# RWKV recurrence on one Trainium2 core: order of the next slot's Gram product, and the engine that masks and copies t1

## The reference, cut to what matters

```python
def frame_step(state, inp):
    r_t, w_t, k_t, v_t, a_t, b_t = inp
    sa = jnp.einsum('bhvk,bhk->bhv', state, a_t)
    state = (state * w_t[:, :, None, :]
             + sa[..., None] * b_t[:, :, None, :]
             + v_t[..., None] * k_t[:, :, None, :])
    y_t = jnp.einsum('bhvk,bhk->bhv', state, r_t)
    return state, y_t
```

## Time and profile before

| | |
|---|---|
| median of 3 runs | 1352.33 us (1350.98 to 1352.74) |
| profiled execution, first to last instruction (the page gives no other time of it) | 1350.7 us |
| PE matmul, weight load | 97%, 84% of the span |
| VectorE, ScalarE, POOL | 70%, 52%, 9% |
| granted TensorE clock | 0.998 |

### The profile page before, as it was taken

How to read it: one execution, slowest core, us unless ns; L and a number is a source line. 1 busy time by engine, 2 the same in 40 slices (tenths; PEclk the granted TensorE clock), 3 DMA queues, 4 the chain that set the end, 5 groups by cost and what they waited for, 6 DMA issues and landing times. The chain is left out here.

```text
span 1350.7 us, 24951 instructions
## 1 busy us (share of the span) xinstructions
PE 1303.9 (97%) x10507; PEld 1130.7 (84%) x10507; DVE 948.4 (70%) x1433; ACT 701.1 (52%) x1211; POOL 128.3 (9%) x133
## 2 busy tenths in 40 slices
PE   4999999999999999999999999999999999999997
PEld 2998888997899887788888887888888998888886
DVE  1887788976768776685556888666657677756655
ACT  2534544434467455564444648654445566644443
POOL 0000000010200864100000142000000021000000
PEclk9999999999999999999999999999999999999999
DMA  9997899995341012356665532465565544565561
GB/s 363 373 366 236 302 350 381 356 344 161 110 156 64 4 35 97 98 178 196 188 192 177 176 121 74 150 203 192 187 196 160 170 143 126 172 188 192 183 197 51
DMA packets 177559, 256.90 MB, mean 190 GB/s; under 512 B 10472, under 2 KB 122536, under 8 KB 177448
## 3 DMA queue, kind: packets, MB, share of 16 engines
q1 hardware_dynamic: 177448, 255.31, 57.0%
HBM read 254.25 MB, written 1.05 MB: 189 GB/s over the span
## 5 line engine op out<-in xcount | busy, mean ns | idle before, releaser
L1507 DVE TENSOR_TENSOR w_lo<-stage,w_hi 128x1024 fp32r<-128x1024 f32 (+1 forms) x372 | 447.3, 1238 | 160.4 <-ACT w_hi L882 160.0
L882 ACT ACTIVATE w_hi<-stage 128x1024 fp32r<-128x1024 f32 (+1 forms) x378 | 379.9, 1049 | 211.7 <-PE acc L2311 191.9
L2309 PE MATMUL acc<-w_hi,z_hi 128*128 128x512 f32 x640 | 252.7, 395 | 1.6 <-DVE z_lo L1956 1.6
L2311 PE MATMUL acc<-w_hi,z_lo 128*128 128x512 f32 x640 | 249.4, 390 | 0.0
L2310 PE MATMUL acc<-w_lo,z_hi 128*128 128x512 f32 x640 | 249.2, 389 | 0.0
L2252 PE MATMUL un<-h_both,w_hi 128*128 128x256 f32 x736 | 214.9, 292 | 1.8 <-POOL w_lo L853 1.1
L2253 PE MATMUL un<-h_both,w_hi 128*128 128x256 f32 x736 | 208.8, 284 | 0.0
L2254 PE MATMUL un<-h_both,w_lo 128*128 128x256 f32 x736 | 208.8, 284 | 0.0
L2252 PEld LDWEIGHTS un<-h_both,w_hi 128*128 128x128 f32 x736 | 141.6, 192 | 9.5 <-issue 5.4
L2309 PEld LDWEIGHTS acc<-w_hi,z_hi 128*128 128x128 f32 x640 | 120.1, 188 | 27.8 <-issue 3.9
L2253 PEld LDWEIGHTS un<-h_both,w_hi 128*128 128x128 f32 x736 | 141.7, 193 | 1.2 <-issue 0.7
(11 more groups left out here) (393 smaller groups left out, 1885.1 us busy)
## 6 DMA issues: line engine op xcount, KB each, us to landing
stage<-in_mlp_w SPq DMA_DIRECT2D x64, 1024.0 KB
ada_buf<-in_ada_w SPq DMA_DIRECT2D x48, 1024.0 KB, 11.1
stage<-in_w_up SPq DMA_DIRECT2D x32, 1024.0 KB
stage<-in_w_down SPq DMA_DIRECT2D x32, 1024.0 KB
stage<-in_conv_w_in SPq DMA_DIRECT2D x12, 1024.0 KB
stage<-in_rw_w_rkv SPq DMA_DIRECT2D x12, 1024.0 KB
stage<-in_w_in_a SPq DMA_DIRECT2D x8, 1024.0 KB
stage<-in_w_kv_b SPq DMA_DIRECT2D x8, 1024.0 KB
```

Of the source, the lines that this page charges most:

```text
L882: A_(w_hi[u % 2][:, half, 0:n], stage[u % NSTAGE][:, half, 0:n], ACT.Copy).then_inc(hi_made, 1)
L1507: V.tensor_tensor(w_lo[u % 2][:, half, 0:n], stage[u % NSTAGE][:, half, 0:n], w_hi[u % 2][:, half, 0:n].bitcast(F32), ALU.subtract).then_i ...
L2309: MM(y, z_hi[:, kt, q], wh[:, i, :], start=(first and kt == 0), stop=False, skip_group_check=True)
L2311: ins = MM(y, z_lo[:, kt, q], wh[:, i, :], start=False, stop=(last and kt == KT - 1), skip_group_check=True)
```

## The change

1. gram is taken apart into gb, start, nb, vt, gk and nk. gb, start (VectorE: level 0 mask, unit added, two turns, for both q at once) and nb (both causal masks, both q at once, 1024 columns) of slot s+1 are steps of slot s: in slots 1 and 2, gb goes ahead of level 5 and start and nb between its t1 and its dx. In slot 0 they follow dx(5,1). gk writes the same two banks as gb, and its masks (nk) are one instruction too, put between dx(2,0) and dx(2,1).
2. The Gram block itself, nb_t, is now t1's left operand at every level, in acc[2], acc[3]. The level's mask is put on the product by VectorE when it copies t1. n_m, POOL's products and ScalarE's t1 copies are gone.
3. The order of the first two levels is mixed with vt, gk and tok; ScalarE's bk_tok copies move from level 1 to level 2; the chain's places are new.
4. keep_y moves from VectorE to ScalarE, behind the copy of u. Places of the beside and group steps are named by step instead of by number. POOL loses its n_m products, and its builds stand first in its list.
5. Elsewhere (near 806 us) a semaphore keys_chosen is replaced by VectorE's own link. The fourth slot's inverse gets a tile of its own.

```diff
-        wkv_prepare = [("gram", 0, 0), ("gram", 0, 1), ("tok", 0, 0), ("tok", 0, 1)]
-        for j in WKV_LEVELS:
+        wkv_prepare = [("vt", 0, 0), ("t1", 1, 0), ("t1", 1, 1), ("gk", 0, 0), ("dx", 1, 0), ("tok", 0, 0), ("dx", 1, 1),
+                       ("t1", 2, 0), ("tok", 0, 1), ("t1", 2, 1), ("dx", 2, 0), ("nk", 0, 0), ("dx", 2, 1)]
+        for j in (3, 4):
             wkv_prepare += [("t1", j, 0), ("t1", j, 1), ("dx", j, 0), ("dx", j, 1)]
-        WKV_CHAIN_AFTER = (0, 1, 1, 5, 6, 8, 11, 12, 14, 16, 18, 20)
+        LAST_LEVEL = [("t1", 5, 0), ("t1", 5, 1), ("dx", 5, 0), ("dx", 5, 1)]
+        NEXT_GRAM, NEXT_START, NEXT_NB = ("gb", 0, 0), ("start", 0, 0), ("nb", 0, 0)
+        LAST_STEPS = ([*LAST_LEVEL, NEXT_GRAM, NEXT_START, NEXT_NB],
+                      [NEXT_GRAM, *LAST_LEVEL[0:2], NEXT_START, NEXT_NB, *LAST_LEVEL[2:4]])
+        WKV_CHAIN_AFTER = (0, 2, 3, 6, 8, 10, 12, 14, 16, 18, 20, 23)
...
+        GROUP_PE = {**{s: {("t1", 3, 1): ("bonus", s - 2), ("dx", 3, 1): ("var", s - 2)} for s in (2, 3)},
+        GROUP_ACT = {**{s: {("t1", 2, 0): (("square", s - 2),), ("t1", 4, 0): (("shift", s - 2),),
+                            ("t1", 4, 1): (("ln", s - 2), ("exp", s - 2), ("square_root", s - 2))} for s in (2, 3)},
+        GROUP_DVE = {**{s: {("dx", 3, 1): (("bonus", s - 2),), ("dx", 4, 1): (("add_eps", s - 2),), ("start", 0, 0) if s == 2 else ("t1", 5, 1): (("root", s - 2),),
+                            ("dx", 5, 1): (("scale", s - 2),)} for s in (2, 3)},
+        CROSSED_AT = ((("dx", 3, 1), ("dx", 4, 1)), (("dx", 4, 0), ("t1", 5, 1)))
+        SPLIT_HIGH = {(0, ("t1", 4, 1)): 0, (0, ("t1", 5, 1)): 1, (1, ("rhs", 2, 0)): 0, (2, ("rhs", 2, 0)): 1}
+        SPLIT_LOW = {(0, ("dx", 4, 1)): 0, (0, ("dx", 5, 1)): 1, (1, ("u", 2, 0)): 0, (2, ("u", 2, 0)): 1}
...
 (POOL)
-                for j in WKV_LEVELS[1:]:
-                        G.tensor_tensor(n_m[(j - 1) % 2][:, q, :, :], nb_t[s % 2][:, q, :, 0:CHUNK],
-                                        level_t[:, j, :].unsqueeze(1).to_broadcast([P, CHUNKS, CHUNK]), ALU.mult).then_inc(nm_ready, 1)
...
 (ScalarE)
                     elif step == "t1":
-                        act.wait_ge(t1_done, 10 * s + 2 * (j - 1) + q + 1)
-                        A_(t1[:, q, :, :], half_bank(acc[q], 0), ACT.Copy).then_inc(t1_out, 1)
-                        if j == 1:
+                        if j == 2:
                             act.wait_ge(tok_done, s + 1)
                             A_(bk_tok[SLOT_SET[s]][:, q, :, :, :].rearrange("p b c s -> p (b c s)"), flat(un[q]), ACT.Copy).then_inc(tok_out, 1)
...
                         A_(wkv_u[:], two_pairs(stat_ps, P), ACT.Copy).then_inc(u_out, 1)
+                        if j:
+                            keep_y(s, j - 1)
+                    elif step == "sy" and j == CHUNKS - 1:
+                        keep_y(s, j)
...
 (VectorE)
+                    if step == "start":
                         dve.wait_ge(g_done, s + 1)
+                        link(V.tensor_tensor(inv_of[s][:], gram_first[:, :, :, 0:CHUNK], in_pairs(level_first), ALU.mult))
+                        link(V.tensor_tensor(inv_of[s][:], inv_of[s][:], in_pairs(eye), ALU.add))
+                        for m in range(2):
+                            if s:
+                                dve.wait_ge(t1_done, 10 * s - 2 + m + 1)
+                            V.transpose(in_line(inv_x[:, m, :, :]), in_line(inv_of[s][:, m, :, :])).then_inc(start_ready, 1)
+                    elif step == "nb":
+                        if s >= 2:
+                            dve.wait_ge(y_done, CHUNKS * (s - 1))
+                        V.tensor_tensor(nb_t[s % 2][:], gram_first, in_pairs(c_("masks")), ALU.mult).then_inc(masked, 1)
+                    elif step == "nk":
                         dve.wait_ge(gk_done, s + 1)
+                        V.tensor_tensor(nk_t[s % 2][:], gram_first, in_pairs(c_("masks")), ALU.mult).then_inc(masked, 1)
+                    elif step == "t1":
+                        dve.wait_ge(t1_done, 10 * s + 2 * (j - 1) + q + 1)
+                        V.tensor_tensor(t1[:, q, :, :], half_bank(acc[2 + q], 0), bc4(level_of[:, j - 1, :], CHUNKS), ALU.mult).then_inc(t1_out, 1)
...
-                        else:
-                            keep_y(s, c)
-                    elif step == "u" and j:
-                        keep_y(s, j - 1)
...
 (PE)
+                    if step == "gb":
+                        pe.wait_ge(built, s + 1)
...
+                            pe.wait_ge(masked, 2 * s)
...
                     elif step == "t1":
+                        if j == 1:
+                            pe.wait_ge(start_ready, 2 * s + q + 1)
+                            pe.wait_ge(masked, 2 * s + 1)
+                            if s:
+                                pe.wait_ge(inv_ready, 10 * s - 2 + q + 1)
+                        else:
+                            pe.wait_ge(inv_ready, 10 * s + 2 * (j - 2) + q + 1)
                         for c in range(CHUNKS):
-                            ins = by_head(half_bank(acc[q], 0)[:, c, :], n_m[(j - 1) % 2][:, q, c, :], xn[:, c, :])
+                            ins = by_head(half_bank(acc[2 + q], 0)[:, c, :], nb_t[i][:, q, c, 0:CHUNK], xn[:, c, :])
...
                             if c == 0:
-                                pe.wait_ge(inv_ready, 12 * s + 12)
+                                pe.wait_ge(inv_ready, 10 * s + 10)
```

More of the change, by code:

```diff
@@ L82, in constant_table @@
     s, q = i[:, None] % CHUNK, np.arange(CHUNK)[None, :]
-    levels = [(s >> (j + 1) == q >> (j + 1)) & ((q >> j) & 1 == 1) & ((s >> j) & 1 == 0) for j in range(6)]
-    put("level_t", np.stack(levels, 1))
+    paired = lambda early, late, j: (early >> (j + 1) == late >> (j + 1)) & ((late >> j) & 1 == 1) & ((early >> j) & 1 == 0)
+    put("level_first", paired(s, q, 0))
+    put("level_of", np.stack([paired(q, s, j) for j in range(1, 6)], 1))
     put("masks", np.concatenate([s < q, s <= q], 1))
@@ L595, in wkv_steps, with step_key @@
         def wkv_steps(slot):
[L597 to L600, removed]
+            if slot == 0:
+                yield from ((step, 0, j, q) for step, j, q in (NEXT_GRAM, NEXT_START, NEXT_NB))
+            if slot == SLOTS:
+                yield from ((step, slot - 1, j, q) for step, j, q in wkv_chain)
+                return
+            for n, (step, j, q) in enumerate(wkv_prepare + LAST_STEPS[min(slot, 1)]):
+                of_next = step in ("gb", "start", "nb")
+                if slot + of_next < SLOTS:
+                    yield step, slot + of_next, j, q
+                if slot:
+                    yield from ((step, slot - 1, c, 0) for (step, c, _), after in zip(wkv_chain, WKV_CHAIN_AFTER) if after == n)
+        def step_key(slot, n, step, j, q):
+            return n if slot == SLOTS else (step, j, q)
         HEAD = (slice(0, HD), slice(HD, P))
@@ L759, in build_bk @@
                 pool.wait_ge(tok_done, s)
+                pool.wait_ge(gk_done, s)
                 t = slice(2 * s, 2 * s + 2)
@@ L1239, in beside_steps @@
                         value_evac(2, stat_ps)
-                    if n == 21:
+                    if n == ("t1", 5, 1):
                         value_evac(3, misc)
-                for half in SPLIT_BESIDE.get((slot, n + 2), ()):
-                    split_half(U_RWO + (slot > 0), half)
+                if (slot, n) in SPLIT_HIGH:
+                    split_half(U_RWO + (slot > 0), SPLIT_HIGH[slot, n])
                 if slot < SLOTS and n in CROSSED_AT[min(slot, 1)]:
@@ L1936, in beside_steps @@
             def beside_steps(slot, n):
-                if slot == 0 and n == 3:
+                if slot == 0 and n == ("vt", 0, 0):
                     split(U_RWV + 3)
@@ L1941, in beside_steps @@
                     dve.wait_ge(chain_input, 3)
[L1942 to L1944 removed]
+                if slot == 0 and n in (("dx", 1, 1), ("dx", 2, 1), ("dx", 3, 1)):
+                    mixer_inputs(3, (n[1] - 1,))
+                if slot == 0 and n == ("dx", 5, 1):
                     dve.wait_ge(unit_done, U_RWV + 4)
[L1946 to L1947 removed]
+                if (slot, n) in SPLIT_LOW:
+                    split_half(U_RWO + (slot > 0), SPLIT_LOW[slot, n])
             bc4 = lambda m, n: m.unsqueeze(1).to_broadcast([P, n, m.shape[-1]])
             in_line = lambda m: m.rearrange("p c s -> p (c s)")
+            in_pairs = lambda m: m.unsqueeze(1).unsqueeze(1).to_broadcast([P, 2, CHUNKS, m.shape[-1]])
             def rw_split(j):
@@ L2703, in _ @@
                         ins.then_inc(dx_done, 1)
-                    else:
+                    elif step in ("rhs", "u", "sy"):
                         c, k = j, CHUNKS * s + j
```

158 lines of the change are left out of this document (64 added, 94 removed).

## The result

The kernel after took 1373.26 us (median of four runs, 1371.15 to 1375.4), the kernel before 1352.26 beside it: a ratio of 1.0158, 95% interval 1.0144 to 1.0172, so 21 us slower. I had forecast 1363.5 and a range up to 1369: the sign was right, the size about half of what came, and the range missed it by 4 us. The profiled execution spans 1371.4 us, 20.7 more than before.

The account below looks back on a forecast made before the run. PE's in-order queue was taken as the bound, through waits at its head: new stalls 20.3 against 11.4 (+8.9), with slot 0 +11.8, less 0.6 for rounding, 1352.3 + 11.2 = 1363.5 us; range 1351 to 1369 for 8 in 10.

Parts of the forecast that it names:

- Part 2: Seams 1 to 2 and 2 to 3: rhs(0) stands 2.4 and 3.1 us for VectorE's inverse adds.
- Seam 0 to 1: gb not moved ahead of level 5; VectorE's list puts t1(1,0) at 5.1 us after gb, PE stands 3.4.
- Part 3: ScalarE's list before u(1) and keep_y holds sy(1): stalls 1.9, 2.5 and 1.4 us in slots 1, 2, 3.
- Part 4: nk behind sy(1): t1(3,1) waits 1.0 us per slot; u(3) 0.7 late in slots 2, 3; slot 1's split 0.7.
- Slot 0: t1 masks wait behind VectorE's mixer and split pieces: +2.9 us, 31 us from gb to gb.
- no contention: Slot 0: if POOL is elsewhere during VectorE's mixer instructions, 1.3 us comes off; no separate chance in the text.
- Clock and DMA must be as before: Condition on the forecast's signs: full clock and almost no DMA, as in the earlier trace; no us given.
- the sum: Recurrence: new stalls 20.3 against 11.4, +8.9; with slot 0 +11.8; 0.6 off for rounding: 1363.5 us.
- A: Faster: seams close if level 5's adds or u(1) come in time; -4.7, 1347.6 us; chance 0.16.
- B: No change: ScalarE's list cheaper, u(1) on time (-5.8), slot 0 covered; 1352 to 1355 us; chance 0.12.
- C: Slower by more: instruction gaps at unhidden places, 1.5 to 3 us more; 1365 to 1370; beyond 1369 chance 0.07.
- D: The change isn't what it says, since slot 0 still ends in the old order; already in the total, no separate chance.

Follow-up runs that it names:

- the filled kernel: Kernel after, with matmuls nobody reads put into seven PE waits, about half as many as in a first try whose fills outlasted the waits: 1367.34 us (1.0113).
- the kernel with the holds: Kernel before, with ScalarE copying u(2) of slots 1, 2 and 3 nine times instead of once: 1360.79 us (1.0071).
- the seam mended: Kernel after, with ScalarE copying t1's Gram half unmasked, VectorE masking only the y half and adding level 5 before turning the new start: 1366.98 us (1.0112).
- the first kernel with gb early in slot 0: Kernel after with all remedies together, and the next Gram product ahead of level 5 in slot 0 too: 1353.15 us (1.0011).

## Why the prediction was right or wrong

**The bound** (PE in order, the wait at its head, each from the list of one engine) held: every wait over 1.4 us in the kernel after is one that the prediction named, with the engine that it named.

**Part 2, seams.** Forecast 2.4 and 3.1 ahead of rhs(0), measured 2.06 and 2.78, ended by the inverse add. Seam 0 to 1: t1(1,0) forecast at gb + 5.1 behind a stand of 3.4; measured 5.32 and 3.43.

**Part 3, sy(1).** Forecast 1.9, 2.5, 1.4; measured 1.82, 2.49, 1.45, ended by keep_y on ScalarE. keep_y itself took 0.67 (0.22 + 0.45), taken at 0.6.

**Part 4.** t1(3,1) forecast 1.0, measured 0.66 in each slot of the filled kernel; u(3) forecast 0.7 in slots 2 and 3, measured 0.72 in slot 2 (0.26 in the filled kernel) and no wait that the timeline lists in slot 3. The 0.7 in level 4 of slot 1 is 0.31 in the filled kernel, ahead of t1(4,0), and the last rhs(0) waits 0.39, forecast 0.5. nb, taken at 1.2, took 1.18 to 1.22.

**Slot 0.** Forecast 31 from gb to gb. With the waits filled it was 31.00, in the kernel after 33.35. VectorE's three mixer instructions beside POOL took 1.28, 1.77 and 1.17; the forecast kept the 1.04 and 1.64 of the earlier trace rows for two and took 0.9 off for what was there before. Its rival, no contention, was worth more than its 1.3: with POOL out of the way the slot fell by 3.2, the drop behind the wait included. The second of the three takes 1.77 beside POOL and 0.69 without it, and the wait ahead of dx(3,0), 2.67 and then 0.95, hung on that; by what mechanism POOL slows VectorE, no run here shows.

**The step that failed** is the sentence "Clock and DMA must be as before", and with it the sum, in which a stall counted once. I wrote down seven new stands of PE of 1.4 to 3.4 us and left the granted clock at the 1.00 of the earlier trace rows. It fell six times. That was worth 5.9 us of the median (filled against after) and 6.7 of the span; without it the time, 1367.34, lies in the range. The kernel before had rows that, held beside the list of stalls, would have suggested a rival "slower by more" by the clock, though not its price. Its mean clock is 0.998 and not 1.00, and outside the slots that I looked at its trace has one drop, behind a wait of 1.06 (PE's timeline, then the window at half clock):

```profile
814.31 0.36 PE L2252 MATMUL un<-h_both,w_hi 128*128 128x256 f32 x1 [1.06 <-POOL w_lo L853]
```
```profile
814.90:818.30 3.40, 3.40 (x19) 3.40 (x18) 2.53 (x6) 0.33 (x2) 3.40 (x5) 0.50 0.04 8
```

**What is left**, 1367.34 against 1363.5, is 3.8. By slot the filled kernel is 31.0, 27.2, 27.8 and 27.7 where I had 31, 26, 27.7 and 26.4. Slot 0 fits. Slots 1 to 3 grew by 10.9 where the sum had 8.9, and that the sum came so near is in part luck, because both of its terms were too large. The new stalls, 20.3, are 15.8 in the timeline of the kernel after (all waits that it lists in slots 1 to 3). The 11.4 set against them is 5.8 when the waits that the timeline of the kernel before lists there are added up: I had got it as length less a count of issue, and the other 5.6 are issue that the count lacked or gaps too small to be listed. 15.8 less 5.8 is 10.0, near the 10.9, so the kernel after has them too. The rest up to 10.9 is in part the fills, where they outlast the wait (sy(1) of slot 1: keep_y ended at 472.39, the fill at 472.75). Beyond these 2.0, 0.6 is what I took off for rounding, without a row for it, and 1.1 is that the medians lie further apart than the spans (15.1 against 14.0); where that comes from is not shown.

**Rivals.** A (faster) hung on VectorE's list at the seam being under 2.6 us; measured it is 4.8, from t1(5,1) at 487.98 to rhs(0). Yet where that list was cut and the Gram product brought forward in slot 0 too, the order paid, as A said, with 0.16% and not 0.35%. B fell with sy(1)'s waits. C looked for its excess in gaps of PE's instructions, and the largest in the filled kernel is 0.46, in slot 1; its own price, 1.5 to 3 us, makes 1365 to 1366.5 and not the 1370 that I wrote. D: slot 0's old order was there, and changing it was worth 3.8.

## What to carry to other kernels

A reorder that moves an engine's list costs where it meets the in-order queue that bounds the kernel: list what the waiting engine's supplier does in order from the last event, and the wait comes out to 0.5 us (2.67 for 2.2 at worst among the large ones here). Add up the waits of both kernels in the same way, from the rows of waits, and not one by a list and the other by what is left of the length. Then ask what TensorE's clock does behind each new wait: here each drop cost 1 to 1.6 us on top, over a quarter of the loss in all. No size of wait can be given as safe from these runs. Before moving masks, look whether a later mask makes an earlier one needless; a plain copy can go to the engine that has time.

## What the runs showed of the hardware that I had not expected

The drop mostly comes behind PE's restart (0.2 to 1.3 us in five of six cases in the kernel after), not in the stand, so the profile's busy share hides it (3.40 of 3.40 us busy at 0.50); PEclk by stretch shows it. It is also not fixed to one wait: the wait of 1.50 at the seam brought a drop in the kernel with the holds and none in the kernel before, and those of 1.83 and 2.49 brought one in the kernel after and none with the seam mended. A drop also came behind a wait of 1.06 in the kernel before, at 814.9, where waits of 1.41 and 1.37, at 556 and 574, brought none, and behind 0.93 and 0.39 in the first kernel with gb early in slot 0. Executions of one kernel differ in it too: 1368.1 us at a mean clock of 0.994 and 1372.4 at 0.989. Its length was 3.4, 6.8 or 10.2 us. Matmuls whose product nobody reads kept the clock at 1.00 through the recurrence and, in the second filled kernel, took 5.9 us off.
